# Gate and up weights interleaved by pairs of k steps and read with a step of two elements, and other places against `hT`

## The reference

```python
def swiglu(x, w_gate, w_up, w_down):
    return (jax.nn.silu(x @ w_gate) * (x @ w_up)) @ w_down

for l in range(DEPTH):
    x = x + 0.5 * swiglu(rms_norm(x, ffn1_norm[l]), ffn1_w_gate[l], ffn1_w_up[l], ffn1_w_down[l])
    h = rms_norm(x, mix_norm[l])
    proj = h @ w_in[l]
    ...
    x = x + merged @ w_out[l]
    x = x + 0.5 * swiglu(rms_norm(x, ffn2_norm[l]), ffn2_w_gate[l], ffn2_w_up[l], ffn2_w_down[l])
```

## Time and profile before

| | us |
|---|---|
| median of 2 runs | 1041.45 (1040.8 to 1042.1) |
| the profiled execution as a run | 1040.86 |
| its span | 1039.1 |
| PE busy in it | 1034.3 |
| PEld, DVE, ACT, POOL busy | 892.9, 718.2, 586.2, 61.7 |

### The profile page before, as it was taken

One profiled execution on the slowest core, in us unless ns is written; L12 is line 12 of the kernel. 1 busy time (PEld: TensorE's weight loads), 2 busy tenths in 40 slices (PEclk: granted clock), 3 DMA queues, 4 the chain that ended last, 5 costly groups with the idle time before them and its releaser, 6 DMA issues.

```text
span 1039.1 us, 15559 instructions
## 1 busy us (share of the span) xinstructions
PE 1034.3 (100%) x5648; PEld 892.9 (86%) x5648; DVE 718.2 (69%) x1132; ACT 586.2 (56%) x935; POOL 61.7 (6%) x71
## 2 busy tenths in 40 slices
PE   9999999999999999999999999999999999999998
PEld 8888888998888888888888888889988888888887
DVE  7766676668786866666687666666688868676665
ACT  7545454557964655454565455454678646454552
POOL 0052000121100000000000000001211000000000
PEclk9999999999999999999999999999999999999999
DMA  7765554455335555655545555634454346545551
GB/s 268 255 230 178 202 167 161 146 187 197 132 123 203 183 191 181 213 182 203 183 152 197 197 201 180 211 133 151 151 204 162 122 162 223 202 164 200 191 172 61
DMA packets 35269, 187.53 MB, mean 180 GB/s; under 512 B 4368, under 2 KB 4384, under 8 KB 20128
## 3 DMA queue, kind: packets, MB, share of 16 engines
q1 hardware_dynamic: 34992, 186.51, 51.6%
q0 software_dynamic: 240, 0.53, 0.2%
HBM read 185.98 MB, written 1.05 MB: 180 GB/s over the span
## 4 chain that ended last, share of the span: by engine, by line
PE 99%; DMA 0%; ACT 0%; DVE 0%; issue 0%; ACTq 0%
PE ps L1369 96%; PE ps L1803 1%; PE ps L1393 1%; PE ps L1832 1%; DMA x_cols<-in_x_first 0%; PE ps L1868 0%; PE ps L1712 0%; ACT hT L610 0%; PE ps L1704 0%; PE ps L1414 0%; DVE x_cols L999 0%; ACT w_hi L554 0%; PE ps L1402 0%; ACTq L609 0%
## 5 line engine op out<-in xcount | busy, mean ns | idle before, releaser
L1369 PE MATMUL ps<-hT,w_hi 128*128 128x512 f32 x1408 | 341.6, 391 | 0.1
L1369 PEld LDWEIGHTS ps<-hT,w_hi 128*128 128x128 f32 x1408 | 258.9, 188 | 51.7 <-ACT w_hi L554 0.4
L884 DVE TENSOR_TENSOR w_lo<-w_raw,w_hi 128x2048 fp32r<-128x2048 f32 x82 | 188.0, 2293 | 87.3 <-ACT w_hi L549 87.3
L1369 PEld LDWEIGHTS ps<-hT,w_lo 128*128 128x128 f32 x1408 | 177.9, 188 | 6.9
L1369 PE MATMUL ps<-hT,w_lo 128*128 128x256 f32 x1408 | 179.7, 279 | 0.0
L1369 PE MATMUL ps<-w_hi,hT 128*128 128x512 f32 (+2 forms) x576 | 174.3, 377 | 0.0
L549 ACT ACTIVATE w_hi<-w_raw 128x2048 fp32r<-128x2048 f32 x85 | 161.9, 1905 | 13.5 <-PE ps L1369 13.2
L1369 PE MATMUL ps<-w_hi,aTl 128*128 128x512 f32 x352 | 137.1, 389 | 0.0
L1369 PE MATMUL ps<-w_lo,aTh 128*128 128x512 f32 x352 | 137.1, 389 | 0.0
L1369 PE MATMUL ps<-w_hi,aTh 128*128 128x512 f32 x352 | 136.8, 391 | 0.0
L578 ACT ACTIVATE S<-ps 128x256 f32<-128x256 f32 x88 | 33.8, 384 | 157.3 <-PE ps L1369 157.3
(11 more groups left out here) (168 smaller groups left out, 953.1 us busy)
## 6 DMA issues: line engine op xcount, KB each, us to landing
w_raw<-in_w_ffn SPq DMA_DIRECT2D x85, 1024.0 KB, 5.0
w_raw<-in_w_ffn SPq DMA_DIRECT2D x90, 512.0 KB, 5.7
w_raw<-in_w_gate SPq DMA_DIRECT2D x16, 1024.0 KB, 5.2
w_raw<-in_w_proj SPq DMA_DIRECT2D x16, 592.0 KB, 4.6
w_raw<-in_w_branch SPq DMA_DIRECT2D x8, 1024.0 KB, 4.8
w_raw<-in_w_out SPq DMA_DIRECT2D x8, 1024.0 KB, 4.9
w_raw<-in_w_uq SPq DMA_DIRECT2D x4, 384.0 KB, 3.0
w_raw<-in_w_ffn SPq DMA_DIRECT2D x4, 256.0 KB, 5.2
```

The lines of the kernel that those rows point to most:

```text
L884: dve.tensor_tensor(wl_gu[b], raw_gu[b], wh_gu[b].bitcast(F32), ALU.subtract).then_inc(lo_gu.sem, 1)
L1369: return pe.matmul(dst, w, m, start=start, stop=stop, skip_group_check=True)
```

## The change

1. In the layout in HBM, which the host prepares, the gate weights and the up weights of each pair of k steps (0 and 1, 2 and 3, ...) are interleaved column by column: column 0 of k = 0, column 0 of k = 1, column 1 of k = 0, and so on. A pair takes 256 elements of a partition as before.
2. All matmuls of gate and up take their 128 stationary columns with a step of two elements, 8 bytes, from that pair.
3. The slots of `w_hi` become 2176 elements wide like those of `w_lo`. The gate and up weights begin at element 0 of their slot in buffer 0 and at element 96 (384 bytes) in buffer 1, both in `w_hi` and in `w_lo`.

The arithmetic, the number of instructions, the semaphores, the DMAs and the order stay the same.

```diff
-LO_SHIFT = 112
-LO_SLOT = GU_COLS + 128
+HI_SHIFT, LO_SHIFT = (0, 96), (0, 96)
+PART_SLOT = GU_COLS + 128
...
-        w_hi = sb("w_hi", [P, MIX_SLOTS * GU_COLS], F32R)
-        w_lo = sb("w_lo", [P, MIX_SLOTS * LO_SLOT], F32R)
...
-        wl_gu = [w_lo[:, i * LO_SLOT + LO_SHIFT:i * LO_SLOT + LO_SHIFT + GU_COLS] for i in range(2)]
...
+        w_hi = sb("w_hi", [P, MIX_SLOTS * PART_SLOT], F32R)
+        w_lo = sb("w_lo", [P, MIX_SLOTS * PART_SLOT], F32R)
+        raw_gu = [w_raw[:, i * GU_COLS:(i + 1) * GU_COLS] for i in range(2)]
+        wh_gu, wl_gu = ([w[:, i * PART_SLOT + at:i * PART_SLOT + at + GU_COLS] for i, at in enumerate(shifts)]
+                        for w, shifts in ((w_hi, HI_SHIFT), (w_lo, LO_SHIFT)))
...
+        mix_hi, mix_lo = ([w[:, i * PART_SLOT:i * PART_SLOT + GU_COLS] for i in range(MIX_SLOTS)] for w in (w_hi, w_lo))
...
+        def gu_col(s, k):
+
+            return (s * KC + k - k % 2) * P + k % 2
...
-                            c = (s * KC + k) * P
-                            high(2 * b + s, wh_gu[b][:, c:c + P], k, k == 0)
+                            c = gu_col(s, k)
+                            high(2 * b + s, wh_gu[b][:, c:c + 2 * P - 1:2], k, k == 0)
...
-                            c = (s * KC + k) * P
-                            ins = low(2 * b + s, wl_gu[b][:, c:c + P], k, k == KC - 1)
+                            c = gu_col(s, k)
+                            ins = low(2 * b + s, wl_gu[b][:, c:c + 2 * P - 1:2], k, k == KC - 1)
...
-        gate, up = (tiles(a[f"{name}_w_{part}"], P).reshape(L, FB, P, KC * P) for part in ("gate", "up"))
+        gate, up = (tiles(a[f"{name}_w_{part}"], P).reshape(L, FB, P, KC // 2, 2, P).swapaxes(4, 5).reshape(L, FB, P, KC * P)
+                    for part in ("gate", "up"))
```

More of the change, by code:

```diff
@@ L110, in build @@
         w_raw = sb("w_raw", [P, MIX_SLOTS * GU_COLS])
-        w_hi = sb("w_hi", [P, MIX_SLOTS * GU_COLS], F32R)
-        w_lo = sb("w_lo", [P, MIX_SLOTS * LO_SLOT], F32R)
-        raw_gu, wh_gu = ([w[:, i * GU_COLS:(i + 1) * GU_COLS] for i in range(2)] for w in (w_raw, w_hi))
-        wl_gu = [w_lo[:, i * LO_SLOT + LO_SHIFT:i * LO_SLOT + LO_SHIFT + GU_COLS] for i in range(2)]
[L115 to L119, removed]
+        w_hi = sb("w_hi", [P, MIX_SLOTS * PART_SLOT], F32R)
[3 more added lines that the diff above has]
+                        for w, shifts in ((w_hi, HI_SHIFT), (w_lo, LO_SHIFT)))
+        raw_d = [w_raw[:, 2 * GU_COLS + i * DN_COLS:2 * GU_COLS + (i + 1) * DN_COLS] for i in range(2)]
+        wh_d, wl_d = ([w[:, 2 * PART_SLOT + i * DN_COLS:2 * PART_SLOT + (i + 1) * DN_COLS] for i in range(2)]
+                      for w in (w_hi, w_lo))
+        mix_raw = [w_raw[:, i * GU_COLS:(i + 1) * GU_COLS] for i in range(MIX_SLOTS)]
+        mix_hi, mix_lo = ([w[:, i * PART_SLOT:i * PART_SLOT + GU_COLS] for i in range(MIX_SLOTS)] for w in (w_hi, w_lo))
         hT = sb("hT", [P, KC, 2, SEQ], F32R)
@@ L1451, in gate_up_low_first @@
                         for k in range(KC):
-                            c = (s * KC + k) * P
-                            low(2 * b + s, wl_gu[b][:, c:c + P], k, False, k == 0)
+                            c = gu_col(s, k)
+                            low(2 * b + s, wl_gu[b][:, c:c + 2 * P - 1:2], k, False, k == 0)
                     for s, sig in enumerate((gate_ps, gu_used)):
                         for k in range(KC):
-                            c = (s * KC + k) * P
-                            ins = high(2 * b + s, wh_gu[b][:, c:c + P], k, False, k == KC - 1)
+                            c = gu_col(s, k)
+                            ins = high(2 * b + s, wh_gu[b][:, c:c + 2 * P - 1:2], k, False, k == KC - 1)
                         ins.then_inc(sig.sem, 1)
@@ L1483, in gate_up_first @@
                             for s in range(2):
-                                c = s * KC * P
-                                low(s, wl_gu[0][:, c:c + P], 0, False, True)
+                                c = gu_col(s, 0)
+                                low(s, wl_gu[0][:, c:c + 2 * P - 1:2], 0, False, True)
                         pe.wait_ge(ht_lo.sem, ht_lo.at(l, 2 * w * KC + k))
                         for s in range(2):
-                            c = (s * KC + k) * P
-                            high(s, wh_gu[0][:, c:c + P], k, False)
+                            c = gu_col(s, k)
+                            high(s, wh_gu[0][:, c:c + 2 * P - 1:2], k, False)
                         if k == 0:
@@ L1507, in start_high_four @@
                             pe.wait_ge(ht_lo.sem, ht_lo.at(0, k))
-                        c = (s * KC + k) * P
-                        high(s, wh_gu[0][:, c:c + P], k, k == 0)
+                        c = gu_col(s, k)
+                        high(s, wh_gu[0][:, c:c + 2 * P - 1:2], k, k == 0)
                 def start_low_four(s, half):
@@ L1517, in start_low_four @@
                     for k in range(4 * half, 4 * half + 4):
-                        c = (s * KC + k) * P
-                        ins = low(s, wl_gu[0][:, c:c + P], k, k == KC - 1)
+                        c = gu_col(s, k)
+                        ins = low(s, wl_gu[0][:, c:c + 2 * P - 1:2], k, k == KC - 1)
                     if half == 1:
@@ L1550, in gate_up_second @@
                         for k in range(KC):
-                            c = (s * KC + k) * P
-                            high(2 + s, wh_gu[1][:, c:c + P], k, k == 0)
+                            c = gu_col(s, k)
+                            high(2 + s, wh_gu[1][:, c:c + 2 * P - 1:2], k, k == 0)
                             if l + w == 0 and s == 1 and k == 4:
```

8 lines of the change are left out of this document (4 added, 4 removed).

## The result

| | before | after |
|---|---|---|
| median, us | 1041.45 | 1052.4 (1051.8 to 1053.0, 2 runs) |
| ratio | 1 | 1.0105, 95% interval 1.0088 to 1.0121 |
| span of the profiled execution | 1039.1 | 1051.2 |

The change costs 11 us, 1.05%, with an interval clear of 1. The time lies inside the stated range (1007 to 1072) and on the other side of the old time than forecast.

What follows compares the result with a forecast made beforehand. The spacing of TensorE's matmuls was taken as the bound. Highs 15.6, slow highs behind the lows 1.3 and lows 12.4 us saved make 29.3, so 1012.2 us; plus 2 for first collisions gave 1014, range 1007 to 1072.

Steps and rivals of the forecast that it cites:

- What bounds the kernel: Whole kernel: TensorE is busy 1034.3 of 1039.1 us, so only the spacing of matmuls can change the time.
- The floor: Gate and up matmuls: least spacing 215.6 ns for highs (512 columns, `w_hi`), 109.0 for lows (256 columns, `w_lo`).
- What the excess is: Large matmuls: beyond a fixed 2.3 ns, the other 9 to 13 ns are a stall caused by the weight load alongside.
- A distance that collides is left after one stall: Gate and up: with the 8-byte step both streams keep their distance, so the stall goes, 29.3 us less; chance 0.42.
- The transposes, the nearest row: Transposes: load and moving operand go at one pace, with only 2.3 ns of excess; taken as model for the change.
- Places: 0 us: Buffers: the new relative places of `hT`, the weights and the rest cost nothing, 0 us.
- The stall grows with the bytes walked: Rival, gate and up: twice the bytes walked by a load doubles the stall, +29.3 us, 1071; chance 0.24.
- The load itself becomes slow: Rival, gate and up loads: a stepped load takes 218 ns, which lows can't hide, +141 us, 1182; chance 0.07.
- Nothing changes: Rival, gate and up: the excess is a fixed price of swapping weights, places and steps don't matter, 1041; chance 0.13.
- 216: Sign in the timeline of a block pair: highs about 216 ns apart, alike in both blocks, if the stall goes.
- 238: Sign in the timeline of a block pair: highs near 238 ns and lows near 127 for a doubled stall.
- even and odd apart: Sign in the timeline: even and odd blocks differ if only one buffer finds a good distance, 1027 to 1041; chance 0.14.

Runs made afterwards that it cites:

- f4: Contiguous loads and places of the kernel before, but the moving operand of gate and up stands still (one column repeated): 1015.3 us.
- f3: Contiguous weight layout of the kernel before, but both the loads and the moving operand of gate and up stand still: 1016.8 us.
- i2: Contiguous loads and places of the kernel before, but the moving operand of gate and up stays within 16 bytes, repeated: 1016.0 us.
- e5: Places of the kernel before, but every gate and up load takes one element 128 times (step 0): 1039.6 us.
- f5: Kernel before with gate and up loading only 64 of the 128 columns for all k but the first: 1042.7 us.
- f6: Kernel before with gate and up loading only 32 of the 128 columns for all k but the first: 1041.2 us.
- e2: Changed kernel with its 8-byte step kept but the places modulo 512 bytes of the kernel before: 1053.8 us, ratio 1.0119.
- e3: Changed kernel, 8-byte step kept, with hT 256 bytes off the weights in buffer 0 and 384 in buffer 1: 1052.7 us.
- h2: Changed kernel, 8-byte step kept, with hT 0 bytes off the high weights and 192 off the low ones: 1051.7 us, ratio 1.0099.
- e1: Changed kernel with the weights contiguous again, keeping the changed places: 1046.0 us, ratio 1.0043.
- i1: 8-byte step of the changed kernel, places of the kernel before, moving operand of gate and up standing still: 1024.7 us.
- g1: Changed kernel made contiguous, hT 64 (buffer 0) and 192 bytes (buffer 1) off the high weights, 192 off the low: 1040.5 us.
- h1: Changed kernel made contiguous, hT 0 bytes off the high weights and 192 off the low ones: 1040.4 us, ratio 0.9993.

## Why the prediction was wrong

- *What bounds the kernel*: right. PE is 100% busy, and the change acted by the spacing of matmuls alone; ACT and DVE kept count and duration (1.91 us copies, 2.30 us subtractions in the groups of after).
- *The floor*: right in size for the highs, 215.6 forecast as lower bound and 215.8 in f4. The lows' 109.0 was never reached; f4 has 111.6.
- *What the excess is*: this is the first step that failed. "A stall that the weight load running beside the matmul causes", by two streams that slide past each other. f3, f4 and i2 show that the highs' excess goes away with the moving operand's walk (215.8) while the load goes on; e5, f5 and f6 show that it doesn't go away with the load's walk or with three quarters of the load (230 to 231). The evidence I read was correct (the excess isn't constant), but it spoke for a dependence on relative place and on the group before, not for the load's walk as the source.
- *"A distance that collides is left after one stall"*: the second, and the term of the sum that decided: -29.3 us, where +11 was measured. Equal paces gave no free distance (e2, e3, h2); the highs of even blocks went up 6.7 ns instead of down 11.1, those of odd blocks up 2.2 instead of down 13.8, the lows up 2.5 instead of down 8.8. The transposes, the nearest row, did not carry over: their load needs 140 ns in the records instead of 188, and their moving operand goes at half pace. The text named both differences and drew nothing from them for the sum. Which of them matters wasn't tried.
- *Places: 0 us.* Wrong for the highs of buffer 1 and the lows: alone the places cost 0.43% (e1). That the downs and the projection would keep their spacing was right for the projection (173.7 for 384 columns in both traces) and for the downs but for the first nine behind a pair (230.9, all 24 together 228.3 in place of 226.7).
- *The rivals.* "The stall grows with the bytes walked" had the sign, with a chance of 0.24. Its price of 29.3 us was 2.7 times too high, and its law is not the right one: step 0 doesn't lower the highs, and a step of 16 bytes doubles the load instead of adding to the stall. "The load itself becomes slow" had the right object for the lows, with a factor of 2 that comes one step later (16 bytes); at 8 bytes the lows go from 111.6 to 117.5 where nothing else holds them (f4, i1). "Nothing changes" falls: the same highs take 226.7 or 233.3 by the pattern of the load beside them. The Trainium skill (TensorE: Matmul & The Clock Gate, section "Step-by-step: what each phase is for") says that loading the next weights takes no read bandwidth from the running matmul. The 6.7 ns are against it.
- *What would show it.* The spacings were the right thing to look at: none of "216", "238" or "even and odd apart" came, but 233, between them.

The range held and the direction did not. That the time fell inside it says little for the mechanism, as the range was drawn wide enough for a rival of the opposite sign.

What stays open: why a matmul with a walking moving operand costs 11 ns more, and whether it would without a load, since every matmul of these runs has a load beside it; why the lows at one distance have two spacings, 113.4 and 117.8; and how exactly the lag of a full load with a step gets into a matmul twice as long as the load.

## What to carry to other kernels

Read a stationary float32r operand contiguously: already every second element makes back-to-back full loads 5% slower and a 512-column matmul beside one up to 6.7 ns, and every fourth doubles the load. Before betting on a mechanism of contention, take each of the two partners away in turn (hold one operand still); here that would have cost two runs and shown that the excess goes with the moving operand's walk and not with the load's. Relative places of operands move single groups by 4 to 6 ns, but what one group gains the next may give back, so only the total time counts.

## What was not expected of the hardware

- A moving operand that stays within 16 bytes streams at 215.8 ns for 512 columns, one that walks through all its columns at 226.7 or more, with a load beside it in both cases.
- Matmuls of 256 columns, each with a full float32r load, stand 111.6 ns apart with contiguous loads and 117.5 with a step of 8 bytes (moving operand still), and 231 with 16 bytes (moving operand walking). The Trainium skill (SBUF — State Buffer, section "Door 1: The DMA port swizzle") says that two hits per line of 16 bytes are enough for full bandwidth. The last figure agrees with it; the second, with two hits, should have been free, and the measurement says 5%.
- The same group at the same distance settles at 113.4 (g1) or at 117.8 ns (h1) with only the places of the high weights changed, and keeps that from the second of its 32 matmuls on.
